# The first head's projections before the token scale of the norm, in a two-block transformer kernel

## The reference

```python
def rms_norm(x, g):
    y = xf * lax.rsqrt(jnp.mean(xf * xf, axis=-1, keepdims=True) + NORM_EPS) * g
n = rms_norm(h, norm_mix[l])
proj = n @ w_in
q_r, fz_f, fz_b, i_r, g_r, q_a, k_a, v_a, gate_r, gate_a = jnp.split(proj, SPLIT_IDX, axis=-1)
qh = jax.nn.silu(q_r) * (HG_KEY_DIM ** -0.5)
f = lb + (1.0 - lb) * jax.nn.sigmoid(z)      # for fz_f and fz_b: keys 1 - f, logs log(f)
```

## Time and profile before

| | |
|---|---|
| median of three runs | 1625.26 us (1623.28 to 1625.79) |
| the profiled execution | 1619.58 us |
| its span on the core | 1617.8 us |
| mean granted clock of TensorE | 0.982 |
| TensorE matmul busy | 1505.2 us, 93% |
| TensorE weight load busy | 1170.7 us |
| VectorE busy | 1042.5 us, 64% |
| GpSimd busy | 856.2 us, 53% |
| ScalarE busy | 472.4 us, 29% |

### The profile page before, as it was taken

The page is one execution under the profiler, slowest core; times in us unless marked ns, Lnnn a source line. Parts: engine busy times, 40 slices in busy tenths (PEclk is TensorE's granted clock), DMA queues, the critical chain, the costliest instruction groups (busy, mean ns, idle before and its releaser), DMA issues.

```text
span 1617.8 us, 20168 instructions
## 1 busy us (share of the span) xinstructions
PE 1505.2 (93%) x6988; PEld 1170.7 (72%) x6988; DVE 1042.5 (64%) x1907; ACT 472.4 (29%) x908; POOL 856.2 (53%) x690
## 2 busy tenths in 40 slices
PE   5989999899999899999999999988989999999996
PEld 3878777566777688678888887865847677666874
DVE  7477797887256632489999982337187788576234
ACT  3455432356212222321011010012252334354111
POOL 3523322433665677266767677673637443433664
PEclk9999999999999999999999999998999999999998
DMA  5211111211332333133333333332413531322331
GB/s 203 79 52 40 40 40 40 65 53 53 105 91 86 90 109 106 53 92 91 92 95 101 93 102 98 103 103 92 129 52 91 104 92 53 117 66 73 123 91 65
DMA packets 38315, 138.48 MB, mean 86 GB/s; under 512 B 4312, under 2 KB 4568, under 8 KB 37592
## 3 DMA queue, kind: packets, MB, share of 16 engines
q1 hardware_dynamic: 33408, 121.65, 24.9%
q10 hardware_dynamic: 4824, 15.69, 3.6%
HBM read 130.51 MB, written 6.82 MB: 85 GB/s over the span
## 4 chain that ended last, share of the span: by engine, by line
PE 77%; DVE 14%; issue 3%; ACT 3%; POOL 1%; PEld 0%; PEldq 0%; DMA 0%; ACTq 0%; DVEq 0%; POOLq 0%
PE pair L528 21%; PE pair L530 20%; PE pair L529 20%; PE pair L768 3%; PE pair L796 3%; PE pair L780 2%; DVE nt L1546 2%; PE pair L622 2%; PE pair L623 1%; DVE rstd L1542 1%; DVE nL L1524 1%; PE pair L984 1%; DVE kk L1737 1%; PE pair L670 1%; POOL wL L485 1%
## 5 line engine op out<-in xcount | busy, mean ns | idle before, releaser
L485 POOL TENSOR_TENSOR wL<-ring,wH 128x1024 fp32r<-128x1024 f32 x228 | 565.9, 2482 | 19.0
L528 PE MATMUL pair<-nH,wH 128*128 128x512 f32 x1120 | 452.4, 404 | 33.3 <-DVE nL L1524 15.4
L530 PE MATMUL pair<-nH,wL 128*128 128x512 f32 x1120 | 440.0, 393 | 0.0
L529 PE MATMUL pair<-nL,wH 128*128 128x512 f32 x1120 | 440.0, 393 | 0.0
L482 POOL TENSOR_TENSOR tick<-tick 128x1 f32<-128x1 f32 x228 | 55.9, 245 | 725.2 <-PE pair L530 716.0
L528 PEld LDWEIGHTS pair<-nH,wH 128*128 128x128 f32 x1120 | 211.8, 189 | 107.9 <-issue 30.0
L530 PEld LDWEIGHTS pair<-nH,wL 128*128 128x128 f32 x1120 | 212.3, 190 | 45.6
L483 POOL TENSOR_SCALAR wH<-ring 128x1024 fp32r<-128x1024 f32 x228 | 243.2, 1067 | 0.0
L529 PEld LDWEIGHTS pair<-nL,wH 128*128 128x128 f32 x1120 | 212.7, 190 | 41.5 <-issue 1.0
L1376 ACT ACTIVATE sgb<-cv 128x512 f32<-128x512 f32 x22 | 14.0, 634 | 208.8 <-DVE cv L1927 208.8
L528 PE MATMUL pair<-aH,wH 128*128 128x512 f32 x176 | 69.7, 396 | 0.0
(11 more groups left out here) (339 smaller groups left out, 2738.9 us busy)
## 6 DMA issues: line engine op xcount, KB each, us to landing
ring<-stream SPq DMA_DIRECT2D x228, 512.0 KB, 3.6
gvec<-gv ACTq DMA_DIRECT2D x1, 2560.0 KB
hT<-xT SPq DMA_DIRECT2D x4, 512.0 KB, 5.4
x_d<-hT ACTq DMA_DIRECT2D x1, 2048.0 KB, 7.8
toep<-gvec ACTq DMA_DIRECT2D x8, 256.0 KB, 3.4
hT<-x_d ACTq DMA_DIRECT2D x1, 2048.0 KB, 8.6
outT<-hT ACTq DMA_DIRECT2D x8, 256.0 KB, 2.2
landing<-const_r ACTq DMA_DIRECT2D x1, 1216.0 KB, 6.3
```

What stands on the lines that cost most here:

```text
L485: pool.tensor_tensor(wL[:, r % SPL, :], ring[:, r, :], wH[:, r % SPL, :].bitcast(F32), ALU.subtract).then_inc(split_done, 1)
L528: mm(out, a[0], b[0], start=first, stop=False)
L529: mm(out, a[0], b[1], start=False, stop=False)
L530: return mm(out, a[1], b[0], start=False, stop=last)
```

## The change

x times its gain alone (without the token factor) is split into xH and xL: ScalarE makes xH as a copy scaled by the gain, beside the squares, and VectorE makes xL = x * gain - xH, beside the additions. Head 0's four projections run on these. Each result is multiplied by rstd when VectorE takes it out of PSUM (`scale_first`), and the sigmoids then work in place. The norm proper, nH and nL, is still made for all later projections. Weight slot 0 is asked for after the first piece of x. TensorE does projection 0 before the sum over the partitions. VectorE's order becomes: xL and additions, rstd, the norm with scale_first(0), (1) and (2) ahead of its chunks 0, 1 and 5, the lower bounds, scale_first(3), the cast, and the recurrence. xH and xL lie over tiles that the recurrence uses later.

```diff
@@ SyncE
             for c in range(0, DC, 2):
                 sp.dma_start(hT[:, c:c + 2, :], xT[:, c:c + 2, :]).then_inc(ld_x[c // 2], 16)
-            for r in range(RAW):
-                if r == 1:
-                    sp.wait_ge(ld_x[-1], 16)
+                if c == 0:
+                    sp.dma_start(ring[:, 0, :], slots[0, 0]).then_inc(landed[0], 16)
+            sp.wait_ge(ld_x[-1], 16)
+            for r in range(1, RAW):
                 sp.dma_start(ring[:, r, :], slots[0, r]).then_inc(landed[r], 16)
@@ TensorE, project and head_step
+                        if ready is not None and c == c0:
+                            pe.wait_ge(ready, k + 1)
-                if j < 4:
+                if j < 4 and h == 0:
+                    project("head0", j, 1, parts(xH, xL, DC), ready=xl_made if j == 0 else None)
...
+            head_step(0, 0)
             norm_sum("mix")
-            for j in range(5):
+            for j in range(1, 5):
@@ ScalarE
-                head_out(0, 3)
...
-            squares("mix", hT, lambda c: act.wait_ge(ld_x[c // 2], 16))
+            for c in range(DC):
+                if c == 0:
+                    act.wait_ge(ld_vec, 16)
+                act.wait_ge(ld_x[c // 2], 16)
+                A(xH[:, c, :], hT[:, c, :], ACT.Copy, scale=vcol("norm_mix", c)).then_inc(xh_made, 1)
+                squares("mix", hT, lambda c: None, chunks=[c])
...
             for j in range(3):
-                head_out(0, j)
+                out_of_bank(act, FIRST["head0"] + j)
+                if j < 2:
+                    A(kk[:, j, 0, :], kk[:, j, 0, :], ACT.Sigmoid).then_inc(first_gated, 1)
+                else:
+                    A(sgb[:, 0, :], qT[:, 0, :], ACT.Sigmoid).then_inc(sg_made, 1)
@@ VectorE, queries and the order
+                    if h == 0:
+                        own(V.scalar_tensor_tensor(out=qT[:, 0, :], in0=qT[:, 0, :], scalar=HG_SCALE, in1=sgb[:, 0, :],
+                                                   op0=ALU.mult, op1=ALU.mult))
+                        return
...
-            accumulate_all("mix")
+            for c in range(DC):
+                dve.wait_ge(xh_made, c + 1)
+                V.scalar_tensor_tensor(out=xL[:, c, :], in0=hT[:, c, :], scalar=vcol("norm_mix", c),
+                                       in1=xH[:, c, :].bitcast(F32), op0=ALU.mult, op1=ALU.subtract).then_inc(xl_made, 1)
+                if c:
+                    accumulate("mix", c)
             inverse("mix")
-            norm("mix", hT, "norm_mix", nH, nL)
+            def scale_first(j):
+                bk, free = product("head0", j)
+                V.tensor_tensor((kk[:, 0, 0, :], kk[:, 1, 0, :], qT[:, 0, :], vraw[:, 0, :])[j], bk, rstd[:, :],
+                                ALU.mult).then_inc(free, 1)
+            def first_beside(c):
+                if c in (0, 1, 5):
+                    scale_first(min(c, 2))
+            norm("mix", hT, "norm_mix", nH, nL, beside=first_beside)
             lower_bounds()
+            scale_first(3)
             dve.wait_ge(ld_r, 16)
             V.tensor_copy(cR[:, :], landing[:, :]).then_inc(zero_one, 1)
```

More of the change, by code:

```diff
@@ L277, in build @@
         kk = place("kk", [P, 2, HG_HEADS, S])
+        vr0 = top[0]
         vr = place("vr", [P, ST, S])
@@ L290, in build @@
         E = place("E", [P, 2, 4, S])
+        xH = place("xH", [P, DC, S], F32R, at=top[0])
+        xL = place("xL", [P, DC, S], F32R, at=vr0)
         X = place("X", [P, 2, 2, LEVELS * P])
@@ L446, in build @@
         t_sc, t_relu, t_acc = sem("t_sc"), sem("t_relu"), sem("t_acc")
+        xh_made, xl_made, first_gated = sem("xh_made"), sem("xl_made"), sem("first_gated")
         gv_done, gv_out = sem("gv_done"), sem("gv_out")
@@ L457, in _ @@
         def _(sp):
+            slots = stream.rearrange("(n r) p m -> n r p m", r=RAW)
             for c in range(0, DC, 2):
                 sp.dma_start(hT[:, c:c + 2, :], xT[:, c:c + 2, :]).then_inc(ld_x[c // 2], 16)
-            slots = stream.rearrange("(n r) p m -> n r p m", r=RAW)
-            for r in range(RAW):
-                if r == 1:
-                    sp.wait_ge(ld_x[-1], 16)
+                if c == 0:
+                    sp.dma_start(ring[:, 0, :], slots[0, 0]).then_inc(landed[0], 16)
+            sp.wait_ge(ld_x[-1], 16)
+            for r in range(1, RAW):
                 sp.dma_start(ring[:, r, :], slots[0, r]).then_inc(landed[r], 16)
@@ L536, in parts, with project @@
                 return [(h[:, k, :], l[:, k, :]) for k in range(n)]
-            def project(stage, c0, n, xs, width=S, inputs=None):
+            def project(stage, c0, n, xs, width=S, inputs=None, ready=None):
                 for c in range(c0, c0 + n):
@@ L545, in project @@
                             r = open_slot()
-                        if inputs is not None and c == c0:
+                        if ready is not None and c == c0:
+                            pe.wait_ge(ready, k + 1)
+                        elif inputs is not None and c == c0:
                             pe.wait_ge(nl_made, SPLIT[inputs] + k + 1)
@@ L597, in head_step @@
             def head_step(h, j):
-                if j < 4:
-                    project(f"head{h}", j, 1, n_parts, inputs="mix" if h + j == 0 else None)
+                if j < 4 and h == 0:
+                    project("head0", j, 1, parts(xH, xL, DC), ready=xl_made if j == 0 else None)
+                elif j < 4:
+                    project(f"head{h}", j, 1, n_parts, inputs="mix" if h == 1 and j == 0 else None)
                 else:
@@ L1295, in _ @@
             act.dma_start(posi[:, :], pos.partition_broadcast(P)).then_inc(ld_pos, 16)
-            highs("mix", nH, DC)
+            for c in range(DC):
+                high("mix", c, nH[:, c, :])
             act.wait_ge(lb_diff, 1)
@@ L1616, in forget @@
                     for d in range(2):
-                        out_of_bank(dve, FIRST[f"head{h}"] + d)
+                        if h:
+                            out_of_bank(dve, FIRST[f"head{h}"] + d)
+                        else:
+                            dve.wait_ge(first_gated, d + 1)
                         own(V.tensor_scalar(lf[:, d, :], kk[:, d, h, :], lb(1, d, h), lb(0, d, h), ALU.mult, ALU.add))
@@ L1858, in _ @@
             dve.wait_ge(ld_vec, 16)
-            accumulate_all("mix")
-            inverse("mix")
-            norm("mix", hT, "norm_mix", nH, nL)
+            for c in range(DC):
+                dve.wait_ge(xh_made, c + 1)
[3 more added lines that the diff above has]
+                    accumulate("mix", c)
+            inverse("mix")
+            def scale_first(j):
[6 more added lines that the diff above has]
+            norm("mix", hT, "norm_mix", nH, nL, beside=first_beside)
             lower_bounds()
+            scale_first(3)
             dve.wait_ge(ld_r, 16)
```

## The result

Over 14 timed runs each, the changed kernel took 1631.51 us in the median (1629.38 to 1642.32), the kernel before 1625.36 (1619.56 to 1631.03). The ratio of the runs is 1.0056, with a 95% interval of 1.0039 to 1.0072: slower by 0.56%, some 9.1 us. The two medians lie 6.2 us apart, the two fastest runs 9.8. 1635.2 was forecast, in a range of 1625 to 1641, with a sum of +9.9 us.

A forecast was written before the change was run, and what follows sets the result against it. It took TensorE's ordered chain from turn_logs to bound the kernel, with VectorE's norm and GpSimd's splits delaying it: +7.9 us, plus 2.0 for the clock, makes +9.9, added to the 1625.3 median: 1635.2 us, range 1625 to 1641.

The forecast's parts named there:

- First product: TensorE's first product of head 0's projections was to start at about 10.5 us instead of 20.95.
- Sums ready: VectorE's sum of squares was to end at 22.8 us, 2.7 of it for split 1; before, 12.5.
- Reciprocal's end: VectorE's reciprocal giving rstd was to end at 28.4 us, 9.8 later than before, with 1.5 for the partition sum.
- Norm: VectorE's first norm was to take 21.4 us: 11.2 own work, 2.1 scalings, 8.1 for three splits; end at 49.8.
- price of 2.7: Cost to VectorE of one GpSimd weight split beside it, 2.7 us, taken from the second norm.
- Behind the norm: VectorE's lower bounds, fourth scaling, cast and maximum were to take 5.6 us, then ScalarE's Ln 1.1.
- Rival (c): ScalarE ends last behind the norm because table switches cost more, 7.8 us against VectorE's 5.6: 1637.4 us; chance 0.04.
- turn_logs: TensorE's transposes of head 0's logarithms were to start at 56.5 us against 48.63, +7.9 us.
- Clock: TensorE's restart after its wait was to run at a low clock, costing head 1 2.0 us.
- Rival (d): TensorE's low clock lasts through head 1's first projection or two, 5.4 or 10.8 us lost: 1638.6 to 1644; chance 0.08.
- The shift stays: From head 1 to the end, the delay of +9.9 us should stay, as later stages depend on no absolute time.
- Rival (e): Weight slot 0 lands as late as before, so no early product; VectorE's path hardly changes: 1634 us; 0.65 with the forecast.

The follow-up runs named there:

- e1: Changed kernel with GpSimd's splits of slot 4 and later held until head 0's forget gates are ready; ratio 1.0071 to the kernel before.
- e7: Kernel before with three unused 128x1024 GpSimd subtractions placed in the norm of x; ratio 1.0056 to the kernel before.
- e4: Changed kernel with 14 unused products filling TensorE's two waits; median 1632.99 us, ratio 1.0035 to the kernel before.
- a1: The changed kernel once more, unedited, profiled a second time; 1629.45 us, beside one run of the kernel before at 1620.12.
- e2: Changed kernel with slot 1's split held until the last addition of squares is done; median 1631.06 us, ratio 1.0033 to the kernel before.
- e3: Changed kernel with the old load order, all of x before weight slot 0; median 1635.36 us, ratio 1.0058 to the kernel before.
- e9: Changed kernel with VectorE's work reordered, slot 5's split held until the norm is done, and three unused products in TensorE's wait for the value; ratio 1.0033.
- e6: Changed kernel with lower bounds and cast in VectorE's wait for the deviation, projection results taken within the norm, splits 1 and 5 held; median 1624.03 us.

## Why the prediction was right

**First product** at 10.5: measured 10.51 and 10.41. **Sums ready** at 22.8: 22.11 and 22.00. Split 1 cost its 2.85 us addition as said, and a pair took 1.27 instead of 1.4. One term was missing and did no harm: ScalarE's first copy had a table load of 1.28 us ahead of it (5.26 in the chain above) and ended at 7.28 instead of 5.5, but the second xL stood behind split 0 anyway and ended at 10.96, as forecast (11.0). **Reciprocal's end** at 28.4: 28.94 and 27.29. The 1.5 taken for the partition sum lies between the two measured, 1.91 and 1.02; both ends of the range occur.

**Norm** of 21.4 us: 21.45 and 21.36. This is the term that decides, and e1 (2.8 a split) and e7 (5.9 for three subtractions in the kernel before) show that what the norm takes beyond its own work is GpSimd's doing. The Trainium skill (SBUF — State Buffer, Who interferes with whom) says why: a VectorE instruction with two SBUF inputs shares a read interface with a GpSimd instruction that reads SBUF, and one with at most one such input, outside the two-port modes, does not contend. The traces agree on both sides. The reciprocal, with one input, takes 3.35 us beside split 2 in after, as much beside split 1 in before, and 3.35 alone at 1606.4 us of before. Of operations that read PSUM, the prediction's example at 42.5 and the scaling at 42.40 of after (0.69) run beside a split's cast only; beside a subtraction stands one at 427.31 of before, 0.69 us, wholly inside a subtraction of 425.86 to 428.49, where the same line takes 0.68 to 0.69 in all its eight executions. The 8-column operation of 0.92, too, stood beside the split's cast (31.25 to 32.30) and not its subtraction, so the cast holds VectorE as well; the price of 2.7 contains both.

**Behind the norm** 5.6 us to the maximum's end and 1.1 for Ln, 6.7 in all: from 50.39 to 57.21 it is 6.8. Rival (c), that ScalarE ends last, falls. Timeline of after, ScalarE:

```profile
51.21 1.28 ACT L1317 ACT_TABLE_LOAD   x1
52.51 1.15 ACT L1317 ACTIVATE kk<-kk 128x512 f32<-128x512 f32 x2
53.56 0.61 ACT L1319 ACTIVATE sgb<-qT 128x512 f32<-128x512 f32 x1
54.19 1.28 ACT L1155 ACT_TABLE_LOAD   x1
56.10 1.06 ACT L1155 ACTIVATE lf<-lf 128x1024 f32<-128x1024 f32 x1 [0.63 <-DVE lf L1641]
```

The Ln table is there at 55.47, 0.6 before VectorE's maximum lets Ln start: near, as the sum had it (5.2 under 5.6). A sigmoid follows its table load within 0.02 us, so the drain that the Trainium skill (ScalarE: Activation LUTs, What ACT_TABLE_LOAD costs) counts with a switch costs nothing here either.

**turn_logs** +7.9: +8.7 and +7.0 against 48.47. **Clock** 2.0: 2.6 and 2.2 (64.22 - 55.48 less 6.55), and e4, which keeps the clock up, shows it by taking it away. Rival (d) asked for 5.4 or more, and falls. Together 9.9 forecast, 11.3 and 9.2 measured at the first gate, and 11.3 and 9.2 again at the product after the rotary angles. **The shift stays**: in a1 it is 9.5 at 1185 us and 9.9 at the end of the span. In the first profile it grows to 21.5; most of that growth lies in low spells of the clock (last section). That 9.9 was forecast and 9.9 is read from a1 is in part luck: turn_logs came 0.9 less late than the sum had it, the clock cost 0.2 more, and 0.7 was added behind the gate, by nothing that the sum holds.

Three steps were rougher than they looked. That the late reciprocal moves everything by its own lateness held only because projection 1 was done by then: in e2 it was not, and a reciprocal 2.7 us earlier than in a1 brought turn_logs 1.6 us later. Rival (e), slot 0 landing late, was said to change the path hardly at all: e3 is that case, and it costs 2.8 us, a fifth split in VectorE's way. And adding the sum to the median, rather than to the profiled execution, gave 1635.2, while after's median is 1631.5: the medians of before and after do not sit at the same place of their spread, and nothing in the profile of before told how wide that is.

## What to carry to other kernels

Work moved ahead on the bound engine is worth nothing by itself if what that engine needs next, in its written order, waits on a serial chain of another engine: read who is late at the first point where it must wait again. An engine that runs ahead frees its buffers ahead, and what refills them (here GpSimd's splits) moves too; look at whom it meets there, and price the meeting in a stretch of the same trace where the two already meet. And an idle spell of the bound engine costs more than its length: 2.2 to 2.6 us are lost to slower products behind it here.

## What the runs showed of the hardware

The granted clock also falls where TensorE has had only short waits, and stays low while it works without a break. The same work in before, in after's first profile, and in a1, in this order:

```profile
177.40:187.40 10.00, 10.00 (x60) 8.88 (x60) 8.60 (x9) 4.76 (x6) 4.15 (x3) 1.00 0.00 0
```

```profile
189.00:199.00 10.00, 10.00 (x36) 8.94 (x36) 5.91 (x10) 1.94 (x2) 0.00 (x0) 0.50 0.00 0
```

```profile
186.80:196.80 10.00, 10.00 (x60) 8.89 (x60) 8.59 (x9) 4.76 (x6) 4.16 (x3) 1.00 0.00 0
```

After's first profile has 36 products in 10 us where the other two have 60, at the clock's lower level, with TensorE busy throughout; a1, the same kernel, has the full clock. Product by product its shift against before grows from 11.6 to 16.4 us over this spell and its edges. Further low stretches, most of all at 250 to 260 us (0.83) and 1448 to 1455 us (0.50), carry it to 21.5. Nothing in TensorE's work ahead of the spell tells the three apart: in the 10.8 us before it the engine is busy for 8.39, 8.35 and 8.33 us, with the same two waits (1.4 and 1.0 us, on VectorE). Run times follow the mean clock: of after's 14 runs eight lie at 1629.4 to 1631.6 with 0.976 to 0.978, and the three at 1641.1 to 1642.3 have 0.968 or 0.969. e1, e4 and e9 brought the first gate forward by 3 to 15 us, and their runs show little of it or nothing. e9's spell, around 56 to 62 us, stands behind a wait of 1.4 us at 53.13, with TensorE busy for 8.09 of the 10.2 us before it. What sets the spells off stays open: e4 and e9 kept TensorE busier, and it did not prevent them. So a gain of a few us at the start of this kernel can be read from one trace and still not be found in a median of ten runs.

The second surprise is how long a small operation can be held: 2.23 us for 8 columns in e6, where 0.92 was the longest in the earlier trace rows. The trace of before has longer ones: two operations on a single column (L1794) that take 2.31 and 2.32 us, where the median of its 32 is 0.16. GpSimd is held in return: its subtraction takes 2.65 to 2.71 us in the norm and 2.40 where VectorE is in the reciprocal.
